# The product of gate and up written to its PSUM bank instead of SBUF, in the feed-forward bodies of a 9-block transformer kernel

## The reference

```python
def swiglu(h, w_in, w_out):
    gate, up = jnp.split(h @ w_in, 2, axis=-1)
    return (jax.nn.silu(gate) * up) @ w_out
```

## Time and profile before

| | |
|---|---|
| median of 3 runs | 2410.27 us (2409.76 to 2411.99) |
| profiled execution | 2406.9 us |
| its span | 2405.0 us |
| mean granted TensorE clock | 0.999 of full |
| TensorE busy | 2329.1 us, 97% |
| VectorE busy | 1577.9 us, 66% |
| ScalarE busy | 910.3 us, 38% |
| GpSimd busy | 1354.8 us, 56% |

### The profile page before, as it was taken

One profiled execution on the slowest core, in us unless ns is written; L12 is line 12 of the kernel. 1 busy time (PEld: TensorE's weight loads), 2 busy tenths in 40 slices (PEclk: granted clock), 3 DMA queues, 4 the chain that ended last, 5 costly groups with the idle time before them and its releaser, 6 DMA issues.

```text
span 2405.0 us, 36289 instructions
## 1 busy us (share of the span) xinstructions
PE 2329.1 (97%) x14528; PEld 2062.9 (86%) x14528; DVE 1577.9 (66%) x2518; ACT 910.3 (38%) x1466; POOL 1354.8 (56%) x700
## 2 busy tenths in 40 slices
PE   7999999999989999999999998899999999999998
PEld 5887789777688777898778897789999999999998
DVE  8999796666679997958983126567527614534661
ACT  4222224455442222233222235554444444545443
POOL 4555455222235554654554443278878887468886
PEclk9999999999999999999999999999999999999999
DMA  7655352211025553534533332145555564345554
GB/s 278 214 189 184 139 206 85 71 54 62 27 88 202 196 182 139 205 109 166 178 129 93 97 90 72 53 149 184 179 156 192 180 189 159 99 145 185 183 179 136
DMA packets 97510, 350.11 MB, mean 146 GB/s; under 512 B 10944, under 2 KB 10944, under 8 KB 96960
## 3 DMA queue, kind: packets, MB, share of 16 engines
q1 hardware_dynamic: 97344, 347.81, 43.2%
HBM read 346.71 MB, written 1.05 MB: 145 GB/s over the span
## 4 chain that ended last, share of the span: by engine, by line
PE 51%; DVE 13%; issue 4%; ACT 2%; POOL 1%; DMA 1%; DVEq 0%; ACTq 0%
PE psum L1555 16%; PE psum L1559 16%; PE psum L1556 16%; DVE psum L1104 7%; PE psum L1904 1%; DVE sq L1321 1%; POOL w_lo L751 1%; PE psum L1876 1%; ACT w_hi L771 1%; DVE gu_hi L1324 0%; DVE psum L1194 0%; DVE h L1200 0%; PE psum L1884 0%; DVE u_lo L1413 0%; DVE pcomb L1386 0%
## 5 line engine op out<-in xcount | busy, mean ns | idle before, releaser
L751 POOL TENSOR_TENSOR w_lo<-w_raw,w_hi 128x1024 fp32r<-128x1024 f32 (+3 forms) x696 | 1354.6, 1971 | 1033.4 <-ACT w_hi L771 1032.7
L1555 PE MATMUL psum<-u_hi,w_hi 128*128 128x256 f32 (+2 forms) x2912 | 975.4, 335 | 16.3 <-POOL w_lo L751 5.3
L1559 PE MATMUL psum<-u_lo,w_hi 128*128 128x256 f32 (+2 forms) x2912 | 947.8, 325 | 3.3 <-DVE u_lo L1186 2.0
L1556 PE MATMUL psum<-u_hi,w_lo 128*128 128x256 f32 (+2 forms) x2912 | 945.8, 325 | 0.0
L771 ACT ACTIVATE w_hi<-w_raw 128x1024 fp32r<-128x1024 f32 (+1 forms) x522 | 529.1, 1030 | 337.7 <-PE psum L1559 275.5
L1555 PEld LDWEIGHTS psum<-u_hi,w_hi 128*128 128x128 f32 x2912 | 553.1, 190 | 98.2 <-issue 25.7
L1559 PEld LDWEIGHTS psum<-u_lo,w_hi 128*128 128x128 f32 x2912 | 552.7, 190 | 52.8 <-DVE u_lo L1186 4.8
L1556 PEld LDWEIGHTS psum<-u_hi,w_lo 128*128 128x128 f32 x2912 | 553.4, 190 | 44.3 <-issue 3.4
L1555 PE MATMUL psum<-gu_hi,w_hi 128*128 128x256 f32 (+1 forms) x1188 | 379.2, 319 | 0.0
L1556 PE MATMUL psum<-gu_hi,w_lo 128*128 128x256 f32 (+1 forms) x1188 | 378.1, 318 | 0.0
L1559 PE MATMUL psum<-gu_lo,w_hi 128*128 128x256 f32 (+1 forms) x1188 | 378.1, 318 | 0.0
(11 more groups left out here) (173 smaller groups left out, 2060.4 us busy)
## 6 DMA issues: line engine op xcount, KB each, us to landing
w_raw<-in_ffn_in SPq DMA_DIRECT2D x264, 512.0 KB, 3.7
w_raw<-in_ffn_out SPq DMA_DIRECT2D x96, 448.0 KB, 3.4
ada_hi<-in_ada_w SPq DMA_DIRECT2D x48, 512.0 KB, 3.6
ada_lo<-in_ada_w SPq DMA_DIRECT2D x48, 512.0 KB, 3.5
w_raw<-in_ffn_out SPq DMA_DIRECT2D x48, 512.0 KB, 3.6
ada_out<-in_ada_w SPq DMA_DIRECT2D x32, 512.0 KB, 4.4
w_raw<-in_b_qkv SPq DMA_DIRECT2D x30, 512.0 KB, 3.4
w_raw<-in_da_in SPq DMA_DIRECT2D x24, 512.0 KB, 3.5
```

The lines of the kernel that those rows point to most:

```text
L751: last = pool.tensor_tensor(w_lo[:, slot, w], w_raw[:, slot, w], w_hi[:, slot, w].bitcast(F32), ALU.subtract)
L1555: mm(out, w_hi[:, slot, w], x_hi, start=start and n == 0, stop=False)
L1556: mm(out, w_lo[:, slot, w], x_hi, start=False, stop=False)
L1559: last = mm(out, w_hi[:, slot, w], x_lo, start=False, stop=stop and n == len(ks) - 1)
```

## The change

The product stays in the bank of the up tile. High and low part are made from there. TensorE's wait ahead of a pair, and ahead of the output, names the low part instead of the product, since the bank is read until then. ScalarE's wait, the ring and the banks are as before.

```diff
+                prod = psum[:, pair_bank(m) + 1, tok]
                 if b["shifted"]:
                     dve.wait_ge(bias_in, 2 * m + 2)
-                    vec.scalar_tensor_tensor(out=s_up[:, j, tok], in0=psum[:, pair_bank(m) + 1, tok], scalar=stat[:, m % 4, 1:2],
+                    vec.scalar_tensor_tensor(out=prod, in0=prod, scalar=stat[:, m % 4, 1:2],
                                              in1=s_up[:, j, tok], op0=ALU.add, op1=ALU.mult).then_inc(g_ready, 1)
                 else:
-                    vec.tensor_tensor(s_up[:, j, tok], s_up[:, j, tok], psum[:, pair_bank(m) + 1, tok], ALU.mult)\
-                       .then_inc(g_ready, 1)
+                    vec.tensor_tensor(prod, s_up[:, j, tok], prod, ALU.mult).then_inc(g_ready, 1)
                 dve.wait_ge(g_ready, FCH * f + m + 1 + PAIR0)
-                vec.tensor_copy(gu_hi[:, m, tok], s_up[:, j, tok]).then_inc(ghi_ready, 1)
+                vec.tensor_copy(gu_hi[:, m, tok], prod).then_inc(ghi_ready, 1)
                 dve.wait_ge(ghi_ready, FCH * f + m + 1)
-                vec.tensor_tensor(gu_lo[:, m, tok], s_up[:, j, tok], gu_hi[:, m, tok].bitcast(F32), ALU.subtract)\
+                vec.tensor_tensor(gu_lo[:, m, tok], prod, gu_hi[:, m, tok].bitcast(F32), ALU.subtract)\
                    .then_inc(gu_ready, 1)
...
-                pe.wait_ge(g_ready, FCH * b["f"] + m)
+                pe.wait_ge(gu_ready, FCH * b["f"] + m)
...
-            pe.wait_ge(g_ready, FCH * b["f"] + 20 + PAIR0)
+            pe.wait_ge(gu_ready, FCH * b["f"] + 20 + PAIR0)
```

## The result

The changed kernel takes 2422.15 us (median of 4 runs, 2421.02 to 2426.12) against 2410.02 for the kernel before (4 runs, 2407.7 to 2411.99). The ratio is 1.0053, 95% interval 1.004 to 1.0065: 0.5% slower. Forecast were 2424.5 us and 0.6%. The profiled execution took 2421.02 us, 14.1 more than that of before (2406.9); the forecast's sum was 14.2. That close a match is partly luck: four runs of one kernel spread over 4 to 5 us.

A forecast was written before the change was run, and what follows sets the result against it. TensorE, 97% busy, bounds the kernel; VectorE sets the pace in modulation stretches. 10.8 + 4.3 - 0.4 - 0.5 = 14.2 us on 2406.9 gives 2421.1, plus 3.4 for the median: 2424.5 us; 8-in-10 range 2416 to 2432.

The forecast's parts named there:

- Product to PSUM: VectorE's product written to PSUM instead of SBUF: 0.5 us at most over 42 turns, taken as nothing.
- Cast out of PSUM: High-part copy in dot-product stretches: 0.686 us instead of 0.43, +0.258 a turn, 42 turns, 10.8 us (bounds 0 and 13.6).
- Low part unchanged: Low part reading PSUM and SBUF instead of SBUF twice: 0.69 us before, 0.68 expected, no change.
- Later release: TensorE waits for the low part: 1.44 us paid once at the last gated pair of three bodies, 4.3 us.
- no new wait arises in the last three bodies: Without dots the low part is done long before the bank is wanted two pairs later, so the release costs nothing.
- Given back: 0.4 us at the first body's start; 0.25 us each from TensorE's GpSimd wait in the fourth and fifth bodies, 0.5 us.
- the sum that I drew from that rule alone: First body's start: all 3.95 us of cast and low-part waits return, total 3.5 us smaller, 2421; held inside the forecast's range.
- the free copy: Rival: the PSUM cast costs no more than the SBUF one, only the shift remains, 2.6 us, 2412.9; chance 0.09.
- the worse order: Rival: order slips the other way or PSUM reads cost more, 0.2 to 0.5 us a turn, 2433 to 2446; chance 0.09.
- The faster rival: GpSimd and VectorE interleave otherwise, one 2.0 us block goes per turn, some 15 us faster, 2395; chance 0.06.
- The point from which it decides: Faster rival's test in modulation turns: the small add would have to come 0.84 us earlier against GpSimd's start.

The follow-up runs named there:

- the split cast: Kernel before, high-part cast still from SBUF but made in four pieces of 128 columns for pairs with dot products: 2418.74 us, ratio 1.0038.
- its own experiment: Kernel before with one edit, TensorE waiting for the low part instead of the product ahead of a pair and the output: 2412.26 us, ratio 1.0008.
- the last fence of the experiments: Changed kernel, with ScalarE making the gate tile's high part only when the third dot of the pair before is done: 2391.75 us, ratio 0.9927.
- Silu early: Changed kernel, with ScalarE's Silu in the 512-token bodies waiting for the product two pairs back instead of its low part: 2424.91 us, ratio 1.0066.
- the rearrangement: Second tile's add behind the low part, gate tile's high part after the previous pair's third dot: changed kernel 2389.72 us, kernel before (product in SBUF) 2389.46 us.

## Why the prediction was right

Point by point, by its own steps:

1. *Product to PSUM, nothing taken.* It takes 691 ns instead of 681, 0.01 us a turn, as allowed.
2. *Cast out of PSUM, 0.686 us, +0.258 a turn.* It is 691 ns against 428: +0.263. The turn is 11.58, forecast 11.57. That the turn grows by just what the cast grows is shown twice, by this kernel and, without PSUM, by the split cast. The estimate from the Trainium skill, "VectorE: DVE Perf Modes", section "Why PSUM operands drop a tier" (0.267 us), is as near.
3. *Low part unchanged.* 691 against 692 ns.
4. *Later release, paid once a body, 4.3 us.* The low parts start later than in the kernel before by 3.48, 9.47 and 13.54 us at the last gated pair of the three bodies, and by 4.94, 10.94 and 15.04 at the end of the body: 1.46, 1.47 and 1.50 us, 4.4 in all. From pair 1 to the last gated pair the same difference grows by 4.30, 4.39 and 2.68 us, 11.4 for the forecast's 10.8 of step 2. In its own experiment the release took 3.5 us in the profiled executions and 1.9 us by the ratio (-0.2 to 4.1), for a forecast of 3.5. There is no price per turn. That no new wait arises in the last three bodies does not hold: see step 5.
5. *Given back, 0.4 and 0.5 us.* The first was mis-sized and small. In the first body, whose start before is in the earlier trace rows, the second product comes at 81.69 us instead of 82.78, so 1.1 us came back where I took 0.4. (In the profile of the change in the first three bodies alone, where GpSimd's tiles came at other times, it was 0.7.) For the second, TensorE's wait of 1.24 us for GpSimd in the fourth body is 0.95, and the one in the fifth 0.88 instead of 1.06: 0.3 + 0.2 us, as forecast. But in the fourth body it is no longer GpSimd that ends the wait; it is the low part of the second pair (1625.50 to 1625.92). So the later release binds there, at the body's start, where I had said that it would not:

```profile
1625.91 0.36 PE L1555 MATMUL psum<-u_hi,w_hi 128*128 128x258 f32 x1 [0.95 <-DVE gu_lo L1326]
```

The start of the first body, DVE and POOL, answers to the earlier trace rows:

```profile
67.96 0.69 DVE L1324 CAST gu_hi<-psum 128x512 fp32r<-128x512 f32 x1
68.69 0.69 DVE L1326 TENSOR_TENSOR gu_lo<-psum,gu_hi 128x512 fp32r<-128x512 f32 x1
...
71.47 3.25 DVE L1104 CUSTOM_DVE_ANT_0 psum<-ada_lo,silu_c 128x1024 f32<-128x1024 f32 x1
74.81 2.18 DVE L1124 TENSOR_SCALAR mcol<-ada_sum,col 128x2 f32<-128x2 f32 x1
...
67.87 9.10 POOL L751 TENSOR_TENSOR w_lo<-w_raw,w_hi 128x1024 fp32r<-128x1024 f32 x3 [19.17 <-ACT w_hi L771]
```

Cast and low part are free of GpSimd, 3.95 us earlier in all. But the dots and the add behind them meet the same subtracts, and most of the gain goes there. Here the Trainium skill, "SBUF — State Buffer", section "Who interferes with whom", agrees with the traces in both halves: cast and low part from SBUF took 2.56 and 2.77 us beside GpSimd, from PSUM 0.69 each. (Only the half on one SBUF input was open before; the last fence of the experiments shows it too.) What fails is the sum that I drew from that rule alone, 3.5 us less: here the block lifted from one instruction fell on the next of its kind.

Of the rivals, the free copy fell with the cast's 691 ns, and the worse order with turns of 11.58. The faster rival did not happen in this change. Its mechanism is real, though: once the subtracts were placed on purpose, the gain was 19 us where I had put its ceiling at 18 and its forecast at 15. The point from which it decides, the order of GpSimd's start against add and dots, was the right one.

Added up from the profiles: 11.4 + 4.4 - 1.1 - 0.5 = 14.2 us, the forecast's number, with a growth 0.6 us larger and a first gain 0.7 us larger that cancel. That part is luck; the mechanism and the two large terms are not.

What stays open: why the medians differ by 12.1 us and the profiled executions by 14.1. The interval of the ratio, 9.6 to 15.7 us, holds both.

## What to carry to other kernels

Find the engine that sets the turn in each stage, and price an edit by what it adds there: 0.26 us on one copy, 42 times over, cost more than 133 us saved on the same engine elsewhere. Moving its source to PSUM slowed the copy (0.43 to 0.69 us for 128x512) and hardly the product (0.01 us), but it takes cast and subtract out of GpSimd's way; the second is worth something only if GpSimd's work is placed beside it. Where two engines exclude each other, first try the order: with one wait on ScalarE and one small step moved, the kernel before became 0.8% faster, and there the product's place no longer mattered.

## What was not expected of the hardware

GpSimd's two subtracts of a turn do not always run back to back. In the turn of the earlier trace rows the first ends at 775.61; the small add that it had held up ends then, and the third dot (775.55, 1.22 us, unstretched) still runs ahead of the second subtract, whose row lasts 3.46 us where one undisturbed has 2.40:

```profile
775.56 3.46 POOL L751 TENSOR_TENSOR w_lo<-w_raw,w_hi 128x1024 fp32r<-128x1024 f32 x1
```

With Silu early, the second dot is the one held up. It runs when the first subtract ends, and then the second subtract (808.61, 3.37 us) goes ahead of the small add. With the rearrangement and the product in SBUF, the cast runs and the second subtract (807.47, 2.58 us) goes ahead of the low part. So the instruction that was held up went next each time, but the one behind it got ahead of GpSimd only in the first case, where it followed without idle time; in the other two VectorE's rows show 0.03 to 0.04 us of idleness in between. No run varies that alone, so what decides the order is not shown. With Silu early or late there were two blocks of about 2 us and the same turn of 11.58.
